# Attention of a hybrid decoder step: the prompt's units in pairs, with the sample's steps between the pairs

## The reference

```python
def win_attention(q, q_pos, k, v, k_pos):
    s = jnp.einsum('btgrd,bkgd->btgrk', q, k) * ATTN_SCALE
    ...
    p = masked_softmax(s, mask)
    return jnp.einsum('btgrk,bkgd->btgrd', p.astype(v.dtype), v)
...
    o = (gates[:, :, 0, :, :, None] * o_cmp + gates[:, :, 1, :, :, None] * o_slc
         + gates[:, :, 2, :, :, None] * o_win)
```

## Time and profile before

| | us |
|---|---|
| median of 3 runs | 1740.98 |
| lowest and highest of the runs | 1733.05, 1743.54 |
| the profiled execution's own time | 1730.56 |
| its span | 1728.9 |
| the attention's stream within it | from 329.3 to 604.1 |
| PE busy in the whole span | 1582.1 (92%) |
| DVE, ACT, POOL busy in the whole span | 764.2, 639.8, 741.3 |

### The profile page before, as it was taken

The page is one execution under the profiler, slowest core; times in us unless marked ns, Lnnn a source line. Parts: engine busy times, 40 slices in busy tenths (PEclk is TensorE's granted clock), DMA queues, the critical chain, the costliest instruction groups (busy, mean ns, idle before and its releaser), DMA issues. The chain is left out here.

```text
span 1728.9 us, 35370 instructions
## 1 busy us (share of the span) xinstructions
PE 1582.1 (92%) x13664; PEld 1397.4 (81%) x13664; DVE 764.2 (44%) x1420; ACT 639.8 (37%) x1186; POOL 741.3 (43%) x522
## 2 busy tenths in 40 slices
PE   6999467698899899999999999998998999999997
PEld 6998466466666688999999988986677999999997
DVE  2211334556556688232232276146658522223235
ACT  2222456355544436322222224136434532222322
POOL 6651453434345555643444327312136644434430
PEclk8999788799999999999999999998999999999999
DMA  8436896355465452533343222234223333233211
GB/s 239 118 82 158 266 294 193 95 183 160 129 188 180 148 181 63 187 118 121 100 128 92 86 73 71 81 91 152 86 69 104 105 103 98 82 91 103 86 33 50
DMA packets 295263, 215.47 MB, mean 125 GB/s; under 512 B 33924, under 2 KB 287416, under 8 KB 294328
## 3 DMA queue, kind: packets, MB, share of 16 engines
q1 hardware_dynamic: 279464, 180.70, 34.7%
q0 software_dynamic: 8496, 22.68, 4.1%
q10 hardware_dynamic: 7136, 9.83, 2.2%
HBM read 200.95 MB, written 20.55 MB: 128 GB/s over the span
## 5 line engine op out<-in xcount | busy, mean ns | idle before, releaser
L1786 POOL TENSOR_TENSOR w_own_t<-w_raw,w_own_t 128x1024 fp32r<-128x1024 f32 (+1 forms) x82 | 194.3, 2376 | 185.2 <-ACT w_own_t L1914 185.2
L1608 PE MATMUL ps<-x_parts,w_own_t 128*128 128x512 f32 x464 | 166.5, 398 | 3.1 <-POOL w_own_t L1786 3.1
L1786 POOL TENSOR_TENSOR w_low_ahead<-w_raw,w_high_ahead 128x1024 fp32r<-128x1024 f32 (+1 forms) x40 | 94.5, 2367 | 129.1 <-ACT w_high_ahead L1914 129.1
L1895 PE MATMUL ps<-x_parts,w_own_t 128*128 128x264 f32 x464 | 132.9, 286 | 0.0
L1896 PE MATMUL ps<-x_parts,w_own_t 128*128 128x264 f32 x464 | 132.4, 285 | 0.0
L1897 PE MATMUL ps<-x_parts,w_own_t 128*128 128x264 f32 x464 | 132.4, 285 | 0.0
L1610 PE MATMUL ps<-x_parts,w_own_t 128*128 128x256 f32 x464 | 130.7, 282 | 0.0
L755 PE MATMUL ps<-flat,w 64*64 64x128 f32 (+1 forms) x2048 | 76.3, 312 | 49.4 <-ACT flat L539 41.6
L1914 ACT CAST w_own_t<-w_raw 128x1024 fp32r<-128x1024 f32 (+1 forms) x82 | 83.4, 1024 | 97.4 <-PE ps L1897 80.4
L755 PEld LDWEIGHTS ps<-flat,w 64*64 64x64 f32 x2048 | 72.1, 156 | 53.9 <-issue 49.4
L2071 DVE TENSOR_REDUCE whole_t<-ps 128x256 f32<-128x512 f32 x44 | 30.4, 690 | 181.2 <-PE ps L1610 181.2
(11 more groups left out here) (450 smaller groups left out, 4838.8 us busy)
## 6 DMA issues: line engine op xcount, KB each, us to landing
w_raw<-in_ffn_w_gu SPq DMA_DIRECT2D x88, 512.0 KB, 3.7
pages<-in_cache_slc SPq DMA_DIRECT2D x192, 128.0 KB
rows<-in_cache_cmp SPq DMA_DIRECT2D x130, 128.0 KB, 5.8
w_raw<-in_ffn_w_down SPq DMA_DIRECT2D x32, 448.0 KB, 3.6
w_raw<-in_gla_w_in SPq DMA_DIRECT2D x24, 512.0 KB, 3.6
rows<-in_cache_cmp POOLq DMA_DIRECT2D x84, 128.0 KB, 6.0
pages<-in_cache_slc POOLq DMA_DIRECT2D x64, 128.0 KB, 2.8
w_raw<-in_ffn_w_down SPq DMA_DIRECT2D x16, 512.0 KB, 4.0
```

What stands on the lines that cost most here:

```text
L1608: nc.tensor.matmul(bank[:, 0:2 * FOLD].rearrange("p (a n) -> p a n", a=2), high, parts[2][:, :, at, 0:FOLD], start=(k == 0), stop=False)
L1786: nc.gpsimd.tensor_tensor(low(u)[:, 0:k], raw[:, u % RAW, 0:k], high(u)[:, 0:k].bitcast(F32), ALU.subtract).then_inc(low_done, 1)
L1895: nc.tensor.matmul(psum(i), high(u)[:, k, :], a[0][:, at, c], start=(k == 0), stop=False)
```

## The change

The prompt's steps are written for pairs of units (n, n+1): both `qk`, then all `turn` of the units n-4 and n-3, then both `pv` of these. The masks of both units come behind the scores of both. A sample's step may stand only behind the second `qk`, the last `turn` or the second `pv` of a pair.

```diff
-    for n in range(U + VLAG + 1):
-        prompt.append(("qk", n, 0, 2.2 * width(n) / 1000 if n < U else 0.0))
-        if TLAG <= n < U + TLAG:
-            for f, part in enumerate(blocks(n - TLAG)):
-                prompt.append(("turn", n - TLAG, f, 0.11 * len(part)))
-        if VLAG <= n < U + VLAG:
-            prompt.append(("pv", n - VLAG, 0, 1.15 * width(n - VLAG) / 1000))
+    for n in range(0, U + LAG + 2, 2):
+        pair = [u for u in (n - LAG, n - LAG + 1) if 0 <= u < U]
+        prompt += [("qk", u, 0, 2.2 * width(u) / 1000 if u < U else 0.0) for u in (n, n + 1)]
+        prompt += [("turn", u, f, 0.11 * len(part)) for u in pair for f, part in enumerate(blocks(u))]
+        prompt += [("pv", u, 0, 1.15 * width(u) / 1000) for u in pair]
+
+    def between(step):
+
+        kind, n, f = step
+        return n % 2 == 1 and (kind != "turn" or f == len(blocks(n)) - 1)
+
...
-        while at_s < len(sample) and took_s / whole_s <= took_p / whole_p:
+        while between(step[:3]) and at_s < len(sample) and took_s / whole_s <= took_p / whole_p:
...
+            def mask(n):
+                t = UN[n][1]
+                for a in range(2):
+                    ins = nc.tensor.matmul(ps[:, SCORE[n % 2] + a, t * P:width(n)], unit[:], above[:], start=False, stop=True)
+                ins.then_inc(qk_done, 1)
+
...
-                for a in range(2):
-                    ins = nc.tensor.matmul(ps[:, SCORE[n % 2] + a, t * P:width(n)], unit[:], above[:], start=False, stop=True)
-                ins.then_inc(qk_done, 1)
+                if n % 2:
+                    mask(n - 1)
+                    mask(n)
...
-                if kind == "qk" and 1 <= n <= U:
+                if kind == "qk" and n % 2 and n < EB:
                     exps(n - 1)
+                    exps(n)
...
-                if kind == "qk" and n > VLAG and UN[n - VLAG - 1][2] == 1:
-                    out_high(n - VLAG - 1)
+                if kind == "qk" and n >= LAG + 2 and n % 2:
+                    out_high(n - LAG - 2)
                 if step in FILL and by_act(step):
                     take(act, nc.scalar.copy, step)
+                if kind == "turn" and n + EB < U and f == len(blocks(n)) - 1:
+                    exps(n + EB)
```

More of the change, by code:

```diff
@@ L956, in phase_attention @@
     NK = QUADS * SUBS
-    TLAG, VLAG, EB = 4, 5, 4
+    LAG, EB = 4, 4
     def width(n):
@@ L1519, in _ @@
                     gate(n - 2)
-                if kind == "qk" and n > VLAG and UN[n - VLAG - 1][2] == 1:
-                    out_low(n - VLAG - 1)
+                if kind == "qk" and n >= LAG + 2 and n % 2:
+                    out_low(n - LAG - 2)
                 if kind == "back":
```

## The result

| | before | after |
|---|---|---|
| median of 4 runs, us | 1738.2 | 1772.4 |
| lowest and highest, us | 1733.1, 1743.5 | 1770.2, 1774.3 |
| the profiled execution's own time, us | 1730.6 | 1774.3 |
| its span, us | 1728.9 | 1772.6 |
| granted clock of TensorE over the whole span | 0.961 | 0.947 |

The changed kernel is slower: the ratio is 1.0203 (95% interval 1.0178 to 1.0227), 34 us in the medians. (The page before was taken from one of its fastest executions, so the two spans differ by 43.7.) The forecast was +20, to 1761 us. The time lies inside the range of 1739 to 1780 us, but above the 1753 to 1768 us that were given to the likeliest case alone.

The account below looks back on a forecast made before the run. PE was taken as the bound. The second stretch's +21.6 (37.5 of new costs, less 7.2 and 8.7) and the first's -1.4 made +20 on the median of 1741.0: 1761 us, range 1739 to 1780.

Parts of the forecast that it names:

- the likeliest case: The forecast itself, new stalls of PE with DVE held by POOL: 1753 to 1768 us alone, chance 0.42.
- Changes of arrangement: PE's switches between array layouts over the stream: 276 before, 181 after, 0.15 us each, 14.3 us saved.
- the waits for `o_raw`: Sample's scores directly behind a second branch's product, nine places before, two after: some 4 of 5.1 us go.
- tile 3, values ahead (less 1.2): Second stretch, pairs with scores of tile 3: fourth fill stalls 2.85 us, less 1.2 covered by the sample's values.
- tile 2 (unit 28): Second stretch, pairs with scores of tile 2, turns of tile 3: PE stalls 2.1 us where uncovered.
- tile 0 (units 42, 43): Second stretch, pairs with scores of tile 0: POOL holds the second gate, the product stalls 3.0 us.
- tile 1: Second stretch, pairs with scores of tile 1: ACT's second copy stands behind exponentials, the last product stalls 1.2 us.
- the pair with "outs": Second stretch: the first "outs" stands between one pair's two maxima, ahead of both copies, adding 3.3 us.
- POOL holds DVE: In tile 0 pairs DVE's second gate waits for POOL's scaling: stall 3.0 us, without it 1.4.
- The clock: Second stretch: long stalls lower PE's clock, 1.5 us at four places, 6.0 together, less 1.5 that goes.
- my third rival: Stalls of 2 to 3 us also lower the clock, eight more pairs at 1.5 us: 1773 us, chance 0.15.
- The rival on the other side: Copies keep ahead, so only the changes of arrangement and `o_raw` waits count: 1723 us, faster, chance 0.13.

Follow-up runs that it names:

- scores alone: The changed kernel with only the scores in pairs; turns and products go singly, each product one unit behind the turn: 1761.0 us.
- products of the pair before: The changed kernel with each pair's products put ahead of the turns of the next pair: 1762.3 us.
- The best version: The changed kernel with DVE's second maximum and gates and POOL's scalings behind the turns, copies by unit, first exponentials and "outs" moved: 1741.3 us.
- the gates together: The changed kernel with both gates of a pair behind both maxima on DVE, without POOL waiting for both: 1797.1 us.

## Why the prediction was right, and where not

**The direction and the mechanism** held: PE lost more in waits for copies than it gained in changes of arrangement. The size was 14 us short in the medians (+34 against +20). My list of waits left out the longest one of before, 3.3 us of the sample's scores for DVE's copy of keys (L1246, near 460.7); it is part of the 14.1 us of idle time, so the sum stays the same.

**Changes of arrangement.** Forecast 95 x 0.15 = 14.3 us; the count of PE's shortest steps gives 14.5. It holds for other numbers of changes too: 44 fewer (scores alone) gave 7.0, 83 fewer (products of the pair before) 12.9, all 0.15 to 0.16 each. But this count has the waits for `o_raw` in it, as said above. A count of the same kind with 0.21 us for the step from a product to the sample's scores gives about 10 us for the 95 changes, 5 for the 44 and 8 for the 83: 0.09 to 0.11 each. So my 0.15, read off one transpose's surroundings, was too high, and some 4 of the 14.5 us are waits for `o_raw` and no changes of arrangement. The gain was never seen in the time by itself either. The waits for `o_raw` went as said, from 5.1 to 1.0 us.

**The stalls per pair** came near to what was worked out at most places, by the distance between starts above the shortest one:

| place | forecast | measured |
|---|---|---|
| tile 3, values ahead (less 1.2) | 1.65 | 1.65 |
| tile 2 (unit 28) | 2.1 | 2.07 |
| tile 0 (units 42, 43) | 3.0 | 2.66 |
| tile 1 | 1.2 | 1.15 |
| the pair with "outs" | 5.4 | 5.4 |
| first stretch, units 14, 16, 22 | 2.2, 2.4, 2.5 | 2.25, 2.76, 2.47 |
| first stretch, unit 24 (three waits) | 4.5 | 4.7 |
| the start | 2.6 | 2.55 |

The other pairs of tile 3 had 1.2 to 1.7. The three covered pairs of tile 2 stalled by 0.5, where 2.1 less 1.2 is 0.9. In the tile 0 pair POOL began 0.25 us behind the start of the first gate's multiplication instead of the 0.44 that I had read off one place, so the hold ended sooner, 3.0 us behind the start of the masks instead of 3.2. In sum the waits are right too: PE's idle time grew by 6.8 and 23.5 us in the two stretches, and I had 4.2 and 25.8 (31.5 of new stalls less 3.4 and 2.3). The pair with "outs" is plain in the order of time of the changed kernel:

```profile
551.59 0.75 DVE L1478 TENSOR_TENSOR og<-ps,gmask 128x256 f32<-128x256 f32 x2
...
554.93 0.96 DVE L1421 TENSOR_REDUCE nmx<-ps 128x2 f32<-128x768 f32 x1
...
556.29 0.68 DVE L1345 COPY pT<-ps 128x512 f32<-128x512 f32 x1
557.12 0.66 PE L1195 MATMUL ps<-ident,e 128*128 128x128 f32 x2 [4.76 <-DVE pT L1345]
```

**POOL holds DVE.** Right in the place and the length: 1.54 us, beside the 1.16 and 0.48 of before, which ended 0.03 and 0.02 us behind POOL's instruction. The Trainium skill's rule ("SBUF — State Buffer", section "SBUF: two separate sides") is borne out in so far as the small multiplication stands still while POOL works: with none and with 32 of them held, two kernels are 42 us apart. That the pair goes to the one that starts first is not borne out by the recorded starts (see the end). The size was low: I had costed it in the five pairs of tile 0 of the second stretch, some 6.7 us of DVE. There it was 16.5 - 38 x 0.16 = 10.4, and the first stretch, for which I gave nothing, had 10.1 - 24 x 0.16 = 6.3 more.

**The clock** is the term that was mis-sized most, and the largest part of the gap. I gave 1.5 us to four places, less 1.5 that goes: +4.5, all in the second stretch. Taking one minus the granted clock times PE's busy time, the second stretch lost 0.10 x 124.5 = 12.5 us against 0.01 x 117.9 = 1.2, the first 0.06 x 123.8 = 7.4 against 0.03 x 123.4 = 3.7: +15.0. (The clock is printed in hundredths, so each product is good to 0.6.) My step was "behind the wait of 2.33 it stayed at 1.00", from a single row, and from that I let stalls of 2 to 3 us in the first stretch and beside covered pairs go free. The rows of the changed kernel above show otherwise. The clock was 0.61 and 0.65 behind waits of 2.7 us at 415.6 and 463.7, 0.69 behind one of 2.33 at 570.8, and 0.57 over 8 us behind one of only 1.45 at 480.0. At the four places to which I had given 1.5 us it was 0.69 at 516.2 and 0.50 at 557.2 and 613.9, but 1.00 behind the 2.59 us at 546.4.

That is my third rival in kind, the clock falling at more places, with the forecast's stalls. It gave 1773 us, and that the median is 1772.4 is in part luck: the rival had eight more pairs at 1.5 us each, while the trace has fewer places with longer drops, and other terms were off as well.

**The rest of the gap.** By stretch: the first +7.2 against -1.4 forecast, the second +30.1 against +21.6, the tail +1.6 against 0: 18.7 in all. The clock is 10.5 of it, the price of a change some 4, and the tail 1.6, with "outs" before the last pair now keeping PE 4.1 us instead of 2.7. That leaves 2 to 3 us, a difference of several small ones. Waits that I had not listed are 2.3 for `x_parts` (L1507, a step of another part that now stands behind two gates on DVE) and 3.0 for two copies of the sample's probabilities. One of these copies, 1.4 us at 480.0, stands in a pair of tile 0 that had its stall in the forecast, so it is not wholly new; and the stalls of tiles 2 and 0 that came out shorter go against them.

**What would show it.** In the second stretch the waits for DVE's copy of `pT` went from 2.3 to 19.3 us (over 20 forecast; in the whole stream from 5.3 to 21.1), the gate of the tile 0 pairs lasts 1.54, the clock is 0.90. One of the signs was ill chosen: PE's busy time in the stream did not fall by 10 to 15 us but rose, from 249.75 to 256.46. Busy time includes work at the half clock, so it mixes the gain and the loss.

**The rival on the other side**, only the changes count, would have needed the chain behind the masks to be short. The best version shows what it takes: another order on DVE, ACT and POOL, and then only no loss.

## What to carry to other kernels

When steps are put together in pairs on the engine that bounds a kernel, the work that its results release on the other engines comes in pairs too, and the first result that is needed stands behind both: write out the other engines' queues before counting what the first one saves. A small instruction that reads two SBUF operands on DVE next to a long one on POOL is a race that hundredths of a microsecond decide; making POOL wait for all of them costs one line. And ask of each queue that issues loads what moved ahead of them: here a later gate on DVE cost 28 us through POOL's page loads.

## What the runs showed of the hardware that I had not expected

- Equal idle times of PE had unequal effects on its clock: 2.59 us ahead of 546.4 left it at 1.00, while stalls of 2.5 to 2.8 us ahead of 415.6, 463.7, 516.2 and 613.9 gave 0.61, 0.65, 0.69 and 0.50 over the next 4 us (1.2 GHz for a good part or all of it, instead of 2.4). A wait of 2.33 us left it at 1.00 in the kernel before and at 0.69 in the changed one at 570.8, and 1.45 us at 480.0 were followed by 0.57 over 8 us. What tells them apart stays open.
- A kernel can get faster by giving PE more to do: 98 unneeded transposes in four stalls took 6.5 us off this one. Part of that may be the drop of the clock at 480.0, which went without being filled.
- The hold between DVE and POOL does not always go to the one that started first. In the kernel before, DVE's `out_low` starts 0.13 us ahead of POOL's scaling and is held until that one ends:

```profile
423.45 2.19 DVE L1430 SCALAR_TENSOR_TENSOR x_parts<-o_raw,x_parts 128x128 fp32r<-128x128 f32 x1 [0.18 <-ACT x_parts L1363]
423.58 1.91 POOL L1148 TENSOR_TENSOR e<-e,rg 128x1024 f32<-128x1024 f32 x1
```

The start in the record need not be the moment at which it reads its operands; alone this instruction takes 0.29 us. With the gates together there is a second case: at 349.75 the second multiplication starts 0.16 us ahead of POOL's scaling (349.91, 0.63 us long) and takes 0.82 us, until that one ends.
